# Sixteen more tokens leave the dense expert projection and are gathered instead

## The reference, cut to what matters

```python
def peer_ffn(h, w_q, keys, u_tab, v_tab):
    q = (ht @ w_q).reshape(t, PEER_HEADS, 2, PEER_HALF)
    sc = jnp.einsum('thid,hikd->thik', q, keys)
    top_s, top_i = lax.top_k(sc, PEER_TOPK)
    cand = top_s[:, :, 0, :, None] + top_s[:, :, 1, None, :]
    best_s, best_pos = lax.top_k(cand.reshape(t, PEER_HEADS, PEER_TOPK * PEER_TOPK), PEER_TOPK)
    i1 = jnp.take_along_axis(top_i[:, :, 0], best_pos // PEER_TOPK, axis=-1)
    i2 = jnp.take_along_axis(top_i[:, :, 1], best_pos % PEER_TOPK, axis=-1)
    experts = i1 * N_KEYS + i2
    gates = jax.nn.softmax(best_s, axis=-1)
    act = einsum('thkd,td->thk', u_tab[experts], h)
    coef = gates * gelu(act)
    return einsum('thk,thkd->td', coef, v_tab[experts])
```

## Time and profile before

| | us |
|---|---|
| median of three runs | 2919.84 |
| lowest, highest | 2913.98, 2921.28 |
| profiled execution: its time | 2915.25 |
| profiled execution: span from first to last instruction | 2913.5 |
| PE busy | 2854.0 (98%) |
| DVE busy | 2495.6 (86%) |
| ACT busy | 1447.4 (50%) |
| POOL busy | 998.9 (34%) |
| DMA, mean over the span | 294 GB/s |

### The profile page before, as it was taken

How to read it: one execution, slowest core, us unless ns; L and a number is a source line. 1 busy time by engine, 2 the same in 40 slices (tenths; PEclk the granted TensorE clock), 3 DMA queues, 4 the chain that set the end, 5 groups by cost and what they waited for, 6 DMA issues and landing times.

```text
span 2913.5 us, 48879 instructions
## 1 busy us (share of the span) xinstructions
PE 2854.0 (98%) x17734; PEld 2666.3 (92%) x17734; DVE 2495.6 (86%) x4773; ACT 1447.4 (50%) x2309; POOL 998.9 (34%) x773
## 2 busy tenths in 40 slices
PE   6999999999999999999999999999999999999998
PEld 4777789999999999999978778999999999999998
DVE  5667789799996899999986779988999879999998
ACT  3345234488883433333353532447888634333333
POOL 1000027644443443444400000675444333443442
PEclk9999999999999999999999999999999999999999
DMA  7435647899999999999931122679999999999996
GB/s 277 169 114 187 255 145 239 304 363 380 393 330 383 360 381 381 382 386 385 379 117 66 66 69 84 200 245 348 394 375 372 345 379 364 387 380 377 378 386 250
DMA packets 261579, 857.75 MB, mean 294 GB/s; under 512 B 25664, under 2 KB 58688, under 8 KB 254784
## 3 DMA queue, kind: packets, MB, share of 16 engines
q1 hardware_dynamic: 158336, 445.11, 41.8%
q0 software_dynamic: 98496, 381.73, 34.9%
q10 hardware_dynamic: 4608, 29.36, 2.4%
...
HBM read 778.50 MB, written 77.59 MB: 294 GB/s over the span
## 4 chain that ended last, share of the span: by engine, by line
PE 83%; DMA 7%; DVE 5%; ACT 3%; issue 2%; SPq 0%; POOL 0%; DVEq 0%; ACTq 0%
PE banks L1037 39%; PE banks L1553 29%; PE banks L1521 4%; DMA w_raw<-wst 4%; PE banks L1358 2%; DMA ring<-u,gidx 2%; PE banks L1053 2%; DVE w_lo L1593 2%; PE banks L1102 1%; ACT w_hi L755 1%; PE banks L1441 1%; DMA pj<-adaw 1%; DVE ring L2087 1%; DVE oneh L2109 1%; PE banks L1199 0%
## 5 line engine op out<-in xcount | busy, mean ns | idle before, releaser
L755 ACT ACTIVATE w_hi<-w_raw 128x1024 fp32r<-128x1024 f32 x596 | 630.3, 1058 | 747.8 <-PE banks L1037 575.0
L1037 PE MATMUL banks<-hH,w_hi 128*128 128x352 f32 (+1 forms) x2528 | 866.4, 343 | 4.8 <-issue 1.7
L1593 DVE TENSOR_TENSOR w_lo<-w_raw,w_hi 128x1024 fp32r<-128x1024 f32 x522 | 638.4, 1223 | 269.8 <-ACT w_hi L755 247.8
L1037 PE MATMUL banks<-hH,w_lo 128*128 128x352 f32 (+1 forms) x2528 | 845.4, 334 | 0.0
L1037 PE MATMUL banks<-hL,w_hi 128*128 128x352 f32 (+1 forms) x2528 | 845.0, 334 | 0.0
L708 POOL DMA_INDIRECT ring<-v,gidx x320 | 396.1, 1238 | 593.0 <-DVE vacc L2099 534.6
L708 POOL DMA_INDIRECT ring<-u,gidx x320 | 399.1, 1247 | 464.7 <-DVE gact L2087 438.9
L1037 PEld LDWEIGHTS banks<-hH,w_hi 128*128 128x128 f32 x2528 | 474.8, 188 | 53.5 <-issue 24.4
L1553 PE MATMUL banks<-c_lo_late,w_hi 128*128 128x352 f32 x1536 | 494.0, 322 | 0.0
L1037 PEld LDWEIGHTS banks<-hH,w_lo 128*128 128x128 f32 x2528 | 474.3, 188 | 19.5
L1037 PEld LDWEIGHTS banks<-hL,w_hi 128*128 128x128 f32 x2528 | 475.1, 188 | 17.4 <-issue 0.5
...
## 6 DMA issues: line engine op xcount, KB each, us to landing
...
activations<-act_out SPq DMA_DIRECT2D x128, 352.0 KB
...
```

The source lines that it names most:

```text
L755: nc.scalar.activation(w_hi[g % 2][:, :, :].rearrange("p a b -> p (a b)"), w_raw[:, g % RAWS, :], ACT.Copy).then_inc(s_wh, 1)
L1037: last = mm(bank[s][:, 0:t.stop - t.start], a[s][:, k, :], b[:, k, t], start=(k == 0 and a is w_hi and b is hH), stop=(k == KT - 1 and a i ...
L1593: v.tensor_tensor(w_lo[g % 2][:, :, :].rearrange("p a b -> p (a b)"), w_raw[:, g % RAWS, :], w_hi[g % 2][:, :, :].rearrange("p a b -> p (a ...
```

## The change

The last 16 of the 352 dense tokens leave the U projection: a tile now has 336 tokens. Their activations come from 16 more gathers of `u_tab` (176 in place of 160 for a layer), each of which serves all 16 tokens: partition s*16+j holds token j with one of its experts. For this PE spreads the routes by one matmul (`tail_rows`), transposes a copied operand into two PSUM banks (`tail_operand`), and DVE makes the row numbers (`tail_gathers`). The 16 sums per slot are put in order by one matmul of 16 columns after tile 89 (`tail_sums`), ACT applies gelu, and DVE multiplies them into the gates of these tokens before their one-hots are made (`tail_coefs`). In the V stage the tokens stay dense: their columns of the gate matrix are already the coefficients and are copied. The V stage's gathers stay 160.

Three more edits come with it. A pick over 16 places for ranks 0 to 7 is cut to 8 places, so each operation of `picked` becomes two. The number of early gathers goes from 14 to 20. The activations of four tiles are one block in DRAM, which a load reads with 5376 contiguous bytes for each partition (before, two pieces of 2816 bytes).

By the tables, gathers used in tiles 37 to 41 go from 7 to 10, in tiles 42 to 101 from 106 to 105, and in tiles 102 to 127 from 33 to 41. The core of the diff:

```diff
@@ constants
+TAIL = 16
+TAIL_SLOTS = P // TAIL
+TU = TD - TAIL
-UG = HK + EXTRA
-GATHERS = 2 * UG
-EARLY_GATHERS = (0, 4, 5, 5)
+VG = HK + EXTRA
+UG = VG + TAIL
+GATHERS = UG + VG
+TAIL_AT = 32
+U_ORDER = [*range(TAIL_AT), *range(VG, UG), *range(TAIL_AT, VG)]
+EARLY_GATHERS = (0, 6, 7, 7)
-POOL_GATHER_AT = [12, 13, 14, 15, 16, 20, 21, 22, 23, 28, 29, 30, 31, 32, 36, 37]
+POOL_GATHER_AT = [11, 12, 13, 14, 15, 16, 17, 18, 19, 20, 21, 24, 25, 26, 27, 29, 30, 31, 33, 34, 37, 38]
 for _n in range(GATHER0, GATE0):
-    U_GATHERS[_n] = 1 if _n % 2 else 2
+    U_GATHERS[_n] = 2
 for _n in range(GATE0, GATE1):
-    U_GATHERS[_n] = 2 if len(quads_of(_n + 1)) < 2 or _n % 4 == 2 else 1
+    U_GATHERS[_n] = 2 if len(quads_of(_n + 1)) < 2 or _n % 16 in (2, 6, 8, 12) else 1
 for _n in range(GATE1, N_KEYS - 1):
-    U_GATHERS[_n] = 2 if _n % 5 in (1, 3) else 1
+    U_GATHERS[_n] = 2 if _n % 8 in (1, 3, 5, 6) or _n == GATE1 + 12 else 1
+U_GATHERS[GATE1 + 2] += UG - EARLY - sum(U_GATHERS)
+TAIL_ROWS, TAIL_SUM, TAIL_MM, TAIL_COEF = GATE0 - 2, 60, 90, 94
...
@@ SP: a group of four tiles is one block of DRAM, a_dram is (GROUPS, P, 2, 2, TU)
-                sp.dma_start(a_dram[p], act_out[:, p % 2, :, :]).then_inc(s_ast[p % 2], 16)
+                sp.dma_start(a_dram[p // 2, :, p % 2, :, :], act_out[:, p % 2, :, :]).then_inc(s_ast[p % 2], 16)
...
-                sp.dma_start(act_in[s][:, :, :, :], a_dram[g * 2:g * 2 + 2].rearrange("q p b t -> p q b t")
-                             ).then_inc(s_ain[s], 16)
+                sp.dma_start(act_in[s][:, :, :, :], a_dram[g]).then_inc(s_ain[s], 16)
@@ ACT
-                    nc.scalar.activation(act_out[:, p % 2, n % 2, :], bank[n % 2][:, 0:TD], ACT.Gelu).then_inc(s_taken, 1)
+                    nc.scalar.activation(act_out[:, p % 2, n % 2, :], bank[n % 2][:, 0:TU], ACT.Gelu).then_inc(s_taken, 1)
...
+                    if n == TAIL_MM:
+                        act.wait_ge(s_tt, l + 1)
+                        nc.scalar.activation(tail_act, bank[4][:, 0:TAIL], ACT.Gelu).then_inc(s_tg, 1)
@@ PE
-                    project(l, U0 + n, s, tokens=slice(TG, T))
+                    project(l, U0 + n, s, tokens=slice(TG, T - TAIL))
...
+                def tail_rows():
+                    pe.wait_ge(s_rt, l * (NT - 1) + NT - 1)
+                    mm(bank[3][:, 0:2 * HK], spread[:, :], route[:, 0:2, :].rearrange("p a j -> p (a j)"),
+                       start=True, stop=True).then_inc(s_xtr3, 1)
+                def tail_operand():
+                    pe.wait_ge(s_htv, l * 2 + 2)
+                    for k in range(KT):
+                        last = nc.tensor.transpose(bank[4 + k // 4][:, k % 4 * P:(k % 4 + 1) * P],
+                                                   tail_src[:, k * P:(k + 1) * P], ident[:, :])
+                    last.then_inc(s_htr3, 1)
+                def tail_sums():
+                    pe.wait_ge(s_tw, l + 1)
+                    mm(bank[4][:, 0:TAIL], tail_wide, tail_token_of[:, :], start=True, stop=True).then_inc(s_tt, 1)
...
-                pe.wait_ge(s_gd, l * GATHERS + HK)
+                pe.wait_ge(s_gd, l * GATHERS + U_PSUM_GATHERS)
@@ DVE
+                tail = slice(T - TAIL, T)
+                link(v.tensor_tensor(h32[:, :, tail], h32[:, :, tail],
+                                     mod[:, 3, :].unsqueeze(2).broadcast_to([P, KT, TAIL]), ALU.add))
+                v.tensor_copy(tail_src[:, :].rearrange("p (k s j) -> p k s j", k=KT, s=TAIL_SLOTS),
+                              h32[:, :, tail].unsqueeze(2).broadcast_to([P, KT, TAIL_SLOTS, TAIL]))
...
-                    link(v.tensor_tensor(pk, at.unsqueeze(2).broadcast_to([P, HK, TOPK]),
-                                         of.unsqueeze(1).broadcast_to([P, HK, TOPK]), op))
+                    boxes = [(slice(0, 8), 8), (slice(8, TOPK), TOPK)]
+                    by_rank = lambda t: t.rearrange("p (h k) -> p h k", h=PH)
+                    for ranks, w in boxes:
+                        box = [P, PH, 8, w]
+                        ins = v.tensor_tensor(pk4[:, :, ranks, 0:w], by_rank(at)[:, :, ranks].unsqueeze(3).broadcast_to(box),
+                                              of[:, 0:w].unsqueeze(1).unsqueeze(1).broadcast_to(box), op)
+                    link(ins)
...
+                def tail_by_slot():
+                    v.tensor_tensor(tail_wide.rearrange("p (s r) -> p s r", s=TAIL_SLOTS),
+                                    gact[:, VG:UG].unsqueeze(1).broadcast_to([P, TAIL_SLOTS, TAIL]),
+                                    tail_slot_of[:, :].unsqueeze(2).broadcast_to([P, TAIL_SLOTS, TAIL]), ALU.mult).then_inc(s_tw, 1)
+                def tail_coefs():
+                    dve.wait_ge(s_tg, l + 1)
+                    link(v.tensor_tensor(idxT[:, 2, TU:TD], idxT[:, 2, TU:TD], tail_act, ALU.mult))
...
-                    v.tensor_tensor(coef[:, b % 2, GSPILL:TD].rearrange("p (c t) -> p c t", c=GKEPT),
-                                    act[:, GSPILL:TD].rearrange("p (c t) -> p c t", c=GKEPT),
-                                    stages[:, :, b, :], ALU.mult).then_inc(s_cp, 1)
+                    v.tensor_copy(coef[:, b % 2, TU:TD], stages[:, 1, b, GWIDE - TAIL:GWIDE])
+                    v.tensor_tensor(coef[:, b % 2, GSPILL:GSPILL + GWIDE], act[:, GSPILL:GSPILL + GWIDE],
+                                    stages[:, 0, b, :], ALU.mult)
+                    v.tensor_tensor(coef[:, b % 2, GSPILL + GWIDE:TU], act[:, GSPILL + GWIDE:TU],
+                                    stages[:, 1, b, 0:GWIDE - TAIL], ALU.mult).then_inc(s_cp, 1)
```

More of the change, by code:

```diff
@@ L213, in sem @@
             return ctx.enter_context(nc.semaphore(name))
+        banks = ctx.enter_context(nc.psum_tensor("banks", [P, 8, T], F32))
+        bank = [banks[:, i, :] for i in range(8)]
         ident = sb("ident", [P, P])
@@ L387, in build @@
         gsum = sb("gsum", [P, 2, PH], where=r2)
+        tail_src = sb("tail_src", [P, D], where=r2)
         r2.close()
@@ L405, in build @@
         sb("ex_to_gates", [P, 18432 - 2 * GSTORED * GROUP * GCHUNK], where=ex)
-        act_in = [sb(f"act_in{s}", [P, 2, 2, TD], where=ex) for s in range(2)]
+        act_in = [sb(f"act_in{s}", [P, 2, 2, TU], where=ex) for s in range(2)]
         c_hi_first = sb("c_hi_first", [P, 2, TD], F32R, where=ex)
@@ L428, in build @@
         before_att.close()
-        banks = ctx.enter_context(nc.psum_tensor("banks", [P, 8, T], F32))
-        bank = [banks[:, i, :] for i in range(8)]
         s_const = sem("const_ready")
@@ L704, in gather @@
                     pool.wait_ge(s_gd, n - RING + 1)
-                if k == HK:
+                col = U_ORDER[k] if k < UG else k - UG
+                if k < UG and col == VG:
+                    pool.wait_ge(s_gidx3, l + 1)
+                if k < UG and col == HK:
                     pool.wait_ge(s_gidx2, l + 1)
@@ L727, in _ @@
                         gather(l, POOL_GATHER_AT.index(n - U0))
-                k = len(POOL_GATHER_AT)
-                used = EARLY
-                for n in range(GATHER0, GATE1):
-                    used += U_GATHERS[n]
-                    if n + 2 in POOL_GATE_LO:
-                        pool.wait_ge(s_wl, l * STREAM + U0 + n + 2)
-                        lo(l, U0 + n + 2)
-                    while k < used + RING:
-                        gather(l, k)
-                        k += 1
-                while k < GATHERS:
+                for k in range(len(POOL_GATHER_AT), GATHERS):
                     gather(l, k)
-                    k += 1
         @block.scalar
@@ L2239, in _ @@
                         extra_gathers()
+                        link(v.tensor_copy(spread[:, :].rearrange("p (s j) -> p s j", s=TAIL_SLOTS),
+                                           ident[:, T - TAIL - 3 * P:P].unsqueeze(1).broadcast_to([P, TAIL_SLOTS, TAIL])))
                 def coefs(b):
```

92 lines of the change are left out of this document (70 added, 22 removed).

## The result

The changed kernel takes 2928.9 us as median (2922.1 to 2933.6), the kernel before 2918.1 (2914.0 to 2921.3) on the same chip. The ratio is 1.0036 with a 95% interval of 1.0025 to 1.0048. The forecast was 2903.5 with a range of 2886 to 2923: it had the sign wrong.

A forecast was written before the change was run, and what follows sets the result against it. PE was taken to lead everywhere by little, DVE or DMA close behind. Terms -3.1 - 10.5 + 2.0 + 0.5 + 1.5 + 0.5 + 1.0 = -8.1 us a layer, -16 in all: median 2903.5, range 2886 to 2923.

The forecast's parts named there:

- Tiles 0 to 37, -3.1: U stage's first 38 tiles: narrower matmuls save 0.082 us a tile in a two-tile loop through POOL's `w_lo`, 3.1 us a layer.
- The slack stays near 10 us: DVE ahead of POOL's last `w_lo`, tiles 0 to 37: shorter picks save 11.0, early gathers cost 7.3, copies and additions about 2.
- I add nothing: POOL's six more issues in tiles 0 to 37: priced at zero; bad end six waits of 2.1 us ahead of `w_lo`.
- Tiles 38 to 101, -10.5 + 1.5: U stage, 64 tiles: PE saves 0.164 us each, 10.5 us a layer; 1.5 lost again, ends 0 and 5.
- PE's added work, +2.0: Spread matmul, eight transposes and the 16-column matmul on PE: 2.0 us a layer, ends 1.7 and 2.6.
- The addition ahead of the search, +0.5: DVE's operand copy and addition ahead of the top-16 search that PE follows: 0.5 us a layer, between nothing and 1.0.
- Tiles 102 to 127, +0.5: Last 26 U tiles: eight more gathers load DMA, 101.8 us taken, 0.5 more than before; possible 98.3 to 111.6.
- V, +1.0: V stage: splitting DVE's product in three adds 0.14 us a tile, which fits; 1.0 us a layer for stalls passed on.
- The rival with 0.15 us for each short operation: V stage: full fixed cost per short operation, 0.58 us for three, DVE overtakes PE; about 2930 us, chance 0.12.
- DMA swallows it: Tiles 102 to 127 at 380 GB/s take 106.5 us, 5 lost in tiles 38 to 101; 2919 us, chance 0.20.
- POOL held: Tiles 0 to 37: six blocked issues of 2.1 us add 12.6 us a layer; 2929 us, chance 0.05.
- All of PE's gain: Only the loop of tiles 0 to 37 limits PE: 15.7 us a layer, perhaps 3 more in V; 2882 us, chance 0.14.

The follow-up runs named there:

- b_early: Kernel before with narrowed picks, 20 early gathers, 24 places for POOL's issues and six late gathers fewer, matmuls still 352 columns: 2914.7 us, 0.9988.
- a_issue: Changed kernel with two more places for POOL's gather issues ahead of tile 38, at tiles 35 and 36: 2924.8 us, 1.0024.
- b_ring4: Kernel before with 4 places in the gather ring in place of 5, no work added: 2940.1 us, 1.0075.
- a_tiny: a_issue with only 8 of 128 partitions fetched by each of the last 41 U-stage gathers, computation incomplete: 2907.6 us, 0.9964.
- a_spread: a_issue with the four V-stage prefetches issued at tiles 110, 113, 119, 122 in place of 110, 112, 114, 116: 2936.7 us, 1.0065.
- b_coef3: Kernel before with only the V stage's 128-column product split into a copy of 16 and products of 64 and 48: 2922.5 us, 1.0016.
- b_narrow: Kernel before with only the U matmuls narrowed to 336 columns, the last 16 tokens lacking their dense part: 2900.9 us, 0.9928.
- b_grouped: Kernel before with only the activations of four tiles as one block in DRAM: 2919.3 us, 1.0001.
- a_flat: a_issue with the gate stage's gathers dealt out over tiles as in the kernel before, same number: 2918.5 us, 1.0004.

## Why the prediction was wrong

- **Where the error lies:** by the profiled executions, 19 of the 27 us between forecast and result stand in tiles 38 to 101 and 6 in the last 26 tiles, both layers together. The 19 are the pause behind tile 38 (13), the price of the columns (5) and smaller things.
- **Tiles 0 to 37, -3.1:** the number was right. Between the same `w_hi` they took 157.7 and 155.7 us for 160.8 and 159.0, -3.2 each. But it came from too high a price of the columns (below); with the measured one the same working gives 2.4, and where the other 0.8 come from is not shown.
- **"The slack stays near 10 us", "I add nothing":** this step failed first. The slack was 2.7 us. Early gathers and picks took 3.7 (b_early), the earlier arrival of PE 3.2, and about 2 are left for the added work. The picks did give their 11.0 (54.9 to 43.6 us from start to start in layer 0). What the sum lacked was that DVE waits for early gathers to land, from 389 to 552 us before and in the changed kernel:
```profile
DVE ring L2087 <- DMA ring<-u,gidx: 0.9, 1, 0.9
```
```profile
DVE ring L2143 <- DMA ring<-u,gidx: 5.3, 2, 5.1
```
  And I priced POOL's issues only as something that blocks `w_lo`. POOL's waits from 389 to 575 us are, beside 5.7 in the earlier trace rows,
```profile
POOL ring L737 <- DVE gact L2143: 6.3, 7, 2.8
...
POOL ring L737 <- DVE gidx L2293: 2.8, 1, 2.8
```
  and since tiles 0 to 37 gave their full 3.2 us they hurt nothing. What hurt was that the gathers which DVE uses ahead of its first `w_lo` were issued between POOL's last two `w_lo` and behind them. It cost 6.0 and 6.9 us. a_issue removes it.
- **Tiles 38 to 101, -10.5 + 1.5:** twice wrong. I interpolated between 512 and 352 columns, 0.0068 us for 16 columns; measured are 0.1586 - 0.1533 = 0.0053, so 0.127 for a tile and 8.1 for 64. The Trainium skill (TensorE: Matmul & The Clock Gate, Back-to-back issue gap) has the isolated gap grow by one cycle of the engine for each column, 6.7 ns for 16 at 2.4 GHz (an estimate from its formula), and says that this formula counts too much at large widths in a stream with weight loads; the trace gives 5.3. And the friction was no 1.5: with the pause behind tile 38 the stretch gave +2.6 and +2.3 us, and without it (a_issue) -0.8 and +0.5. I had looked at DVE's busy share (95.7% now). What the traces show in its place is the turn of the ring, with gathers that land after 14.6 us in the median beside the gate stores; b_ring4 shows how little room this stage has for it: with one place fewer it takes 10 us more. Narrowing alone gave 5.6 and 2.4 in tiles 42 to 101.
- **PE's added work, +2.0:** about 1.4. The spread matmul takes 0.43 us (565.34 to 565.77), the eight transposes 0.79 (566.10 to 566.89), the matmul of 16 columns 0.14.
- **The addition ahead of the search, +0.5:** the stage of the query projection took 1.2 us more in layer 0 and 0.1 in layer 1. The six kernels derived from the one before all stay within 0.1 us of it in layer 0.
- **Tiles 102 to 127, +0.5:** the mechanism was right and the sum named its price, 103.4 us at 410 GB/s; I then took 1.6 off for gathers waiting in the ring. Measured are 104.2 us at 402 GB/s in layer 0 and 105.3 in layer 1, so +2.9 and +3.7. The mean rate hid that ACT waits up to 5.2 us for a single load of weights, and PE then pays the lower clock too. That the gathers' transfers are what delays it is shown (a_tiny); the part of the large prefetches is argued from a_spread.
- **V, +1.0:** +1.7 and +1.8. b_coef3's interval shows a real cost of 0.06 to 0.26%. But b_narrow (+1.7, +2.9) and b_early (+2.1, +0.7) have longer V stages than the profiled execution of before, without touching V's code, so how much of it is the split stays open. Each load of activations shrinks by 32 KB (704 to 672), not by the 64 that the prediction has; b_grouped puts the worth of the layout at nothing. The rival with 0.15 us for each short operation fell (0.33 for three).
- **Rivals:** *DMA swallows it* is the nearest: it had 106.5 us for the last stretch, where 104.2 and 105.3 came, and its range of 2910 to 2930 holds the result, in part by the pause behind tile 38, which it did not have. *POOL held* gave 2929, the number that came, but that is luck: its blocked issues never stood in PE's way. *All of PE's gain* fell already with b_narrow.
- **The signs I had named:** the 336-column spacing (0.153 for 0.152), two tiles in 7.7 us near tile 20 and DMA over 400 GB/s came as forecast; tiles 42 to 101 in 305 us for 301 and the last 26 tiles in 104 for 102 did not. The condition for "wrong" that I had set on POOL, over 10 us, was not met (6.3 + 2.8): it watched the wrong thing.

In round numbers, from the timed runs: the narrower matmuls give 21 us (0.72% by the ratio), picks and early gathers about 3, the split in V takes 5 (2 to 8), and the layout nothing. If these add up, some 30 us are left as what 16 more gathers a layer cost with this order of work. About 4 go with the issue places, and 6 between a_issue and a_flat (both by ratios whose intervals nearly touch or overlap). By the profiled executions the last 26 tiles are 4.6 and 5.6 us longer than in b_narrow, 10 in all; a_tiny against a_issue has 17 us for all 41 late gathers there, not only the new ones. The other 10 are not placed. The mixer stages are 0.3 and 1.9 us longer than before, but the profiled executions of the six kernels derived from the one before reach up to 1.3 and 1.7 us more as well.
